# A conv and retention block on eight cores: keys of two pairs opened without the shift, loads in that order, and retention's first four chunks reordered with factors for eight heads at once

## The reference, cut to what matters

```
xm = rmsnorm(x, norm_w) * (1 + sc_x) + sh_x       # sh_x, sc_x: first two thirds of silu(c) @ ada_w + ada_b
q, k, v, gates = split(xm @ w_in)                 # the same weights for the 256 context tokens (cm)
q, k = rope2d(q), rope2d(k * 64 ** -0.5)          # 8 heads of 64; v has 8 heads of 128
s_f, s_b = states of the context's k, v           # start of the scans, forward and backward
ret = scan_forward(q, k, v, s_f) + scan_backward(q, k, v, s_b)     # chunks of 128 tokens
ret_n = (ret - mean) * rsqrt(var + eps) * gn_w    # per head
y_a = (silu(za) * bg * (conv3(cg * h) + conv_b)) @ w_a
y_b = (silu(zb) * ret_n) @ w_b
out = rmsnorm(x + g_x * ((sigmoid(ga) * y_a + sigmoid(gb) * y_b) @ w_out), final_norm_w)
```

## Time and profile before

| | us |
|---|---|
| median of 3 runs (lowest 876.34, highest 927.11) | 877.23 |
| the profiled execution's own time | 877.3 |
| its span on the slowest core (core 0) | 875.7 |
| spans of the 8 cores | 870.9 to 875.7 |
| PE busy within the span | 800.4 |
| DVE, ACT, POOL busy | 465.4, 360.7, 330.8 |

### The profile page before, as it was taken

How to read it: one execution, slowest core, us unless ns; L and a number is a source line. 1 busy time by engine, 2 the same in 40 slices (tenths; PEclk the granted TensorE clock), 3 DMA queues, 4 the chain that set the end, 5 groups by cost and what they waited for, 6 DMA issues and landing times.

```text
span 875.7 us, 14323 instructions; the slowest of 8 cores (870.9 to 875.7 us)
## 1 busy us (share of the span) xinstructions
PE 800.4 (91%) x4504; PEld 384.6 (44%) x4504; DVE 465.4 (53%) x1090; ACT 360.7 (41%) x642; POOL 330.8 (38%) x372
## 2 busy tenths in 40 slices
PE   0079999999988999999999999999999999999996
PEld 0045445444444444444444444444444444444443
DVE  2457534899778777767623442344256412333435
ACT  3589646898466435343432122122212211222222
POOL 0136523676578454545410302221143143232333
PEclk9999999999999999999999999999999999999999
DMA  8999955774391221315551715325015260034233
GB/s 244 280 290 187 212 111 97 175 156 104 55 162 35 38 54 29 55 29 78 81 86 42 118 34 96 52 46 97 1 23 122 81 112 1 25 118 148 72 120 145
DMA packets 72256, 87.83 MB, mean 100 GB/s; under 512 B 51691, under 2 KB 57963, under 8 KB 70518
## 3 DMA queue, kind: packets, MB, share of 16 engines
q1 hardware_dynamic: 66854, 59.65, 25.9%
q0 software_dynamic: 5328, 27.27, 18.9%
HBM read 93.72 MB, written 8.39 MB: 117 GB/s over the span
## 4 chain that ended last, share of the span: by engine, by line
PE 80%; DMA 6%; ACT 5%; DVE 4%; issue 3%; POOL 1%; SPq 1%; DVEq 0%; ACTq 0%; POOLq 0%
PE P L1006 53%; PE P L588 13%; PE P L1303 6%; DMA wt<-ada_w 4%; ACT tm L983 2%; DMA cm<-rope 2%; PE P L707 2%; DVE vb L1021 1%; ACT st L905 1%; PE P L828 1%; PE P L648 1%; PE P L946 1%; PE P L475 1%; PE P L691 1%; PE P L947 1%
## 5 line engine op out<-in xcount | busy, mean ns | idle before, releaser
L1006 PE MATMUL P<-xmt,vb 128*128 128x512 bf16 x1280 | 283.1, 379 | 2.8 <-DVE wt L1202 1.8
L1006 PEld LDWEIGHTS P<-xmt,vb 128*128 128x128 bf16 x1280 | 124.5, 98 | 152.6 <-issue 3.7
L588 PE MATMUL P<-wt,xmt 128*128 128x512 bf16 x688 | 158.3, 382 | 4.4 <-ACT xmt L509 3.4
L1006 PE MATMUL P<-xmt,wt 128*128 128x512 bf16 x512 | 118.8, 380 | 1.1 <-ACT wt L1157 0.9
L1205 POOL TENSOR_TENSOR kz<-tm,wt 128x1024 bf16<-128x1024 f32 x16 | 45.7, 2857 | 162.4 <-DVE wt L1202 162.4
L588 PEld LDWEIGHTS P<-wt,xmt 128*128 128x128 bf16 x688 | 65.2, 98 | 79.8 <-issue 7.5
L1006 PEld LDWEIGHTS P<-xmt,wt 128*128 128x128 bf16 x512 | 49.3, 98 | 58.3 <-issue 2.7
L1282 DVE SCALAR_TENSOR_TENSOR tm<-tm,P 128x512 f32<-128x512 f32 x32 | 22.0, 687 | 87.6 <-PE P L1006 87.6
L1158 DVE TENSOR_TENSOR wt<-P,wt 128x512 f32<-128x512 f32 x32 | 22.1, 692 | 83.4 <-ACT wt L1157 62.8
L1284 POOL TENSOR_TENSOR st<-st,tm 128x512 bf16<-128x512 bf16 x32 | 39.8, 1243 | 65.8 <-DVE tm L1282 65.8
L1006 PE MATMUL P<-vb,wt 128*128 128x512 bf16 x256 | 61.4, 386 | 0.0
(11 more groups left out here) (176 smaller groups left out, 1110.8 us busy)
## 6 DMA issues: line engine op xcount, KB each, us to landing
kz<-x SPq DMA_DIRECT2D x24, 512.0 KB, 9.2
wt<-x SPq DMA_DIRECT2D x24, 512.0 KB, 4.6
vb<-w_conv POOLq DMA_DIRECT2D x16, 512.0 KB, 8.3
out<-wt SPq DMA_DIRECT2D x15, 512.0 KB, 2.7
st<-ada_w SPq DMA_DIRECT2D x2, 2048.0 KB, 14.1
wt<-ada_w SPq DMA_DIRECT2D x2, 2048.0 KB, 28.8
vb<-w_mix POOLq DMA_DIRECT2D x8, 512.0 KB, 11.1
cm<-rope SPq DMA_DIRECT2D x33, 64.0 KB, 3.9
```

The costliest lines, as they stand in the source:

```text
L588: ins = e.matmul(pf(bank)[:, 0:wid], lhsT=lhs_x(ch, k), rhs=w[:, k, c0_:c0_ + wid], start=(k == 0), stop=(k == 7))
L1006: ins = e.matmul(pf(bank), lhsT=lhs(k), rhs=rhs(k), start=(k == 0), stop=(k == 7))
```

## The change

It has two parts; lines are those of the kernel before.

**A. The start.** The blocks of ada_w are loaded and multiplied in the order 2, 3 (scale), then 0, 1 (shift). w_k is loaded by SP as two float32 pieces (`wk_load`) and cast on DVE and ACT (`wk_cast`) instead of by one casting DMA of POOL. With the scale known and the shift not, pairs 0 and 1 are written as `xm` without the shift (`f_aff_noshift`), and their keys are begun in banks P2 to P5 (`k_open`, four chunks of 8 products). When the shift is there, it is split into two bf16 parts (`shi`), multiplied with w_k into P6 (`f_kb`, 8 products with 2 rows), split again (`kbh`, `kbl`) and added to each of the four banks by two products with ones (`k_close`). Then follow the ropes of the four chunks, and the loop begins at p = 2, where `g_acc` is called for pairs 0 and 1 both. The two columns `xmTh` that the convolution needs are made from `xh2`. The exponents of the mask are made before ada block 0 is cast (`mask_exponents`), the rest after pair 1 is opened. Loads of pairs 2, 3 and 4 follow the last ada block.

**B. Retention.** In chunks 1 to 3 the next queries' products stand in front of the scores, the first filler in front of `r_ret`, the norm is split in two around it, and only one filler is left behind `r_ret`; then `r_rtp` and `r_qtp` follow each other. In chunk 0 `r_qtp(1)` stands in front of `r_ret(0)`. `r_qtp(0)` uses bank P4 instead of P0. In all 16 chunks the factors are made for eight heads at once instead of twice for four.

SP's queue at the start, before. `ada_w` rows are blocks of 2 MB, `x` rows are chunks of 512 KB with a count, `st`, `wt`, `kz`, `xmt`, `cm` and `tm` are regions of SBUF.

The diff, cut:

```diff
+        def f_aff_noshift(pair):
+            ...
+            P.op("dve", f_d, reads=["Amod", "P0"], writes=[n_ + "d" for n_ in names])
+            P.op("act", f_a, reads=["Amod", "P1"], writes=[n_ + "a" for n_ in names])
...
+        ada_load(2)
         load2(0)
+        ada_load(3)
+        wk_load(0)
+        wk_load(1)
+        P.dma("sp", lambda e: e.dma_start(out=dpn, in_=dpn_d[:, :]), "dpn", writes=["dpn"])
+        load2(1)
+        ada_load(0)
         rope2(0)
         rope2(1)
+        ada_load(1)
+        ada_cast(2)
+        ada_mm(2, 7, 0)
+        load2(2)
+        rope2(2)
+        load2(3)
+        sq2(0)
+        scale2(0)
+        load2(4)
+        f_tp(other[0])
...
+        ada_cast(3)
+        ada_mm(3, 7, 0)
+        modT_part((1,), "modT1", 7, 0)
...
+        wk_cast(0)
+        f_aff_noshift(other[0])
+        wk_cast(1)
+        def k_open(ch, bank, part):
+            def f(e):
+                for k in range(4 * part, 4 * part + 4):
+                    ins = e.matmul(pf(bank), lhsT=lhs_x(ch, k), rhs=wk[:, k, :], start=(k == 0), stop=False)
...
+        def k_close(bank):
+            def f(e):
+                e.matmul(pf(bank), lhsT=onesb[0:2, :], rhs=kbh[0:2, :], start=False, stop=False)
+                return e.matmul(pf(bank), lhsT=onesb[0:2, :], rhs=kbl[0:2, :], start=False, stop=True)
...
+        for part in range(2):
+            for c in range(2):
+                k_open(other[0][c], 2 + c, part)
+        mask_exponents()
+        sq2(1)
+        scale2(1)
+        load2(5)
+        f_tp(other[1])
         ada_cast(0)
         ada_mm(0, 7, 0)
+        f_aff_noshift(other[1])
+        for part in range(2):
+            for c in range(2):
+                k_open(other[1][c], 4 + c, part)
+        mask_tables()
         ada_cast(1)
         ada_mm(1, 7, 0)
+        modT_part((0,), "modT", 7, 0)
...
+        P.op("dve", f_shi, reads=["modT"], writes=["shi"])
+        P.op("dve", f_slo, reads=["modT", "shi"], writes=["shi"])
...
+                ins = e.matmul(pf(6)[0:2, :], lhsT=shi[:, k, :], rhs=wk[:, k, :], start=(k == 0), stop=(k == 7))
...
+        P.op("dve", lambda e: e.tensor_copy(out=kbh[0:2, :], in_=pf(6)[0:2, :]), reads=["P6"], writes=["kbh"])
...
+        for c in range(4):
+            k_close(2 + c)
...
-        for p in range(8):
+        for c in range(2):
+            o_krope(other[0][c], 2 + c)
+        rope2(3)
+        sq2(2)
+        scale2(2)
+        o_krope(other[1][0], 4)
+        f_tp(other[2])
+        f_aff(other[2])
+        o_krope(other[1][1], 5)
...
+        for p in range(2, 8):
...
-            if p >= 1:
-                g_acc(other[p - 1], range(4), 4, p == 1, False)
+            if p == 2:
+                g_acc(other[0], range(4), 4, True, False)
+            g_acc(other[p - 1], range(4), 4, False, False)
...
+            P.op("dve", f_bna, reads=["bst0", "bst1"], writes=["bmv0", "bmv1"])
...
+            P.op("pool", lambda e: e.tensor_tensor(out=rstd8, in0=rstd8, in1=neghalf[:, 0:8], op=ALU.pow),
+                 reads=["rstd0", "rstd1", "neghalf"], writes=["rstd0", "rstd1"])
...
-        r_qtp(0)
+        r_qtp(0, 4)
...
+            if n < 4:
+                if n:
+                    r_q(n + 1, 5, rest=False)
+                r_sc(n)
+                if n:
+                    r_q(n + 1, 5, pe=False)
+                    r_norm(n - 1, (0,))
+                first_filler(n, 0)
+                if n:
+                    r_norm(n - 1, (1,))
+                else:
+                    r_qtp(1)
+                r_ret(n)
+                first_filler(n, 1)
+                if n:
+                    r_rtp(n - 1)
+                r_Fadd(n + 1)
+                if n:
+                    r_qtp(n + 1)
+                else:
+                    first_filler(0, 2)
+                continue
```

156 lines of the change are left out of this document (91 added, 65 removed).

## The result

The changed kernel takes 891.86 us (median of 4 runs, 890.38 to 892.09), the kernel before 877.16 us in the same session. The ratio is 1.0167, with a 95% interval of 1.0154 to 1.018. In some runs the cores of one die are slower as a whole at a lower granted clock; all ratios here leave such runs out. I had forecast 875.5 us, with a range of 872.0 to 880.5: the change costs 14.7 us where I had expected it to gain 1.7. It stays within 2%, as forecast, but far outside the range.

A forecast was written before the change was run, and what follows sets the result against it. PE was taken to bound all but a few places, so gains lay only where it stands still. From 877.3: start 0, early chunks -1.2, factors for eight heads -0.6, giving 875.5 us, range 872.0 to 880.5.

The forecast's parts named there:

- ACT's squares of pairs 2 and 3: Start: squares wait for x landing 3.4 and 6.7 us after the last ada block, yet finish before PE needs them.
- The landing L: Start: time the last ada block lands, forecast to move from 42.3 by +4.1 us to 46.4.
- SP is passed by nothing it needs: Start: loads of pairs 2 to 4, now queued before the last ada block's landing, keep the DMA engines busy after it.
- above 49: Start: sign of being wrong, the last ada block landing later than 49 us; below 44 was the other side.
- The chain behind L: Start: steps from the last ada block's landing to pair 2's first product, 15.5 us, ending at 61.9.
- the fast level: Start: PE's pace assumed for the eight shift products, 1.73 us instead of 3.53 at the slow level.
- a rival that had the slow one: Start: PE at its slow level when the shift arrives, with transfers 1.5 us slower; 880.0 us, chance 0.25.
- the wait at P0: Retention, chunks 1 to 3: queries' transposes wait for ACT to read bank P0; PE stands still 1.65 us.
- Chunk 4's scores: Retention: scores of chunk 4 start at 274.9 against 276.15, a term of -1.2 us.
- The power for eight heads: Retention: POOL's power for all eight heads at once takes 2.5 us, 0.6 longer, beside DVE's state addition.
- the sum of -1.8: Part B, retention: -1.2 us from the early chunks and -0.6 from factors for eight heads.
- all rivals taken together: Whole kernel: slow PE 880.0, chance 0.25; short wait at P0 872.2, chance 0.20; no effect 876.5, chance 0.15.

The follow-up runs named there:

- the chunks alone: Part B only (new chunk order, factors for eight heads) put on the kernel before, with its old start; 879.59 us, ratio 1.0027.
- The reordered start: Changed kernel with last ada block ahead of rope rows, pairs 2 and 3's scalings and pair 2's transposes and affine step moved earlier; 883.32 us, ratio 1.007.

## Why the prediction was wrong

**The step that failed** is this one of part A: "ACT's squares of pairs 2 and 3 need x that lands 3.4 and 6.7 us after L, and are done before PE asks for them by this timetable." The squares were done, 4 us after the block came. But `sq2` issues two POOL instructions per chunk as well, and I had not looked at what stands ahead of them in POOL's order. In the code written out anew, `o_krope` of pair 0 came first, and with it decay products that wait for the shift. I had listed the queues that SP was moved past, and left POOL's out. Pair 2's product came at L + 22.25, not L + 15.5; with two calls moved it comes 5.1 us earlier in the mean of the cores, and the time falls by 4.8.

**The landing L** was mis-sized: +4.1 forecast (46.4), +7.3 measured (49.57). The bytes were counted about rightly (with the order put right it is +5.1 on the slowest core and +4.6 in the mean of the cores); SP's issue was not. Three small rope rows held SP for 11.47 us, so the last ada block, of 2 MB, was issued at 24.82. With the block ahead of them it was cast at 47.35, so 2.2 of the 3.2 missing are the order (2.4 in the mean of the cores). I had given SP's order a sentence ("SP is passed by nothing it needs") and not a time. I had named "above 49" as a sign of being wrong.

**The chain behind L** held where PE's clock didn't enter: `modT_part` at L + 3.11 (forecast 3.15), the shift products at L + 3.98 (4.05), two reads at 0.68 each (0.65), the rotations 1.99 apart (1.94), the affine step 1.37 (1.36). The shift products took 3.25 us, not 1.73, so the closing began at L + 8.94 and not L + 7.5. I had chosen the fast level against a rival that had the slow one, since sixteen opened products stood "shortly before"; here they ended 5.2 us before the shift products began, with waits of 3.24 and 0.98 us between. The rival's mechanism came, but it ended at 880.0, because it counted opened, shift and closing products alone. The slow level went on with the idleness: pair 2's first products took 3.57, transposes twice 1.86, another eight products 2.78, in sum 4.2 us over the fast times between 67 and 81 us, where the granted clock was 0.53. From pair 2 to pair 3 it took 12.68 and not 7.8. The slow shift products are a consequence and not a cause of their own: with the last ada block issued ahead of the rope rows, and no edit to the products, they take 1.89 on six cores of eight, in after on one.

**What came back**: the loss was 14.45 us at pair 3 and 11.90 at the first scores. Why 2.5 are regained between them no run tested.

**Part B, the chunks**: the wait at P0 was forecast at 1.65 and measured at 1.31 to 1.47, a chunk at 9.0 and measured at 8.87; the scores' wait is gone except in chunk 4, as said. Chunk 4's scores were to gain 1.2, 0.3 of it ahead of chunk 0; from chunk 0 to chunk 4 they gained 0.57 and not 0.9, since the first chunk took 9.49 and not 8.7. The power for eight heads was forecast at 2.5 and takes 2.55 in chunk 4; the gate starts 0.46 sooner in its chain, not 0.2, but it counts at one gate and not at three. So the parts of part B were right within 0.8 us, and the sum of -1.8 was wrong by 4.2 (the chunks alone cost 2.4). Most of that are things that I had not counted at all. One is the clock: I moved a wait to stand next to another, and PE fell to 1.2 GHz behind both, 1.69 us, on five of the eight cores of the chunks alone. The other is the collision, 1.64 us and as much again for the clock behind it (2.87 between the scores), which my text had even described, in the citation on the wide power, but which I looked for at one pair of instructions only. Against them stands a gain that I hadn't counted either: before's own collision, at the second gate, is gone, 1.66 us.

**The chances**: all rivals taken together reached from 872.2 to 880.0. None was a queue behind a waiting instruction. The reordered start, which changes nothing but the order of calls, gives 8.5 of the 14.7 us back by the ratios, so the larger part of the loss is order. That the time still stayed within 2% of before, as forecast, owes nothing to the sum.

## What to carry to other kernels

- When a call is moved, write down every instruction that it issues on every engine, and for each what now stands ahead of it in that engine's order and what that waits for. The small instruction on the idlest engine (here two of under 0.6 us on POOL, which had been idle for 24 us) is the one to look for first.
- A wait of PE can cost more than itself. Here PE ran slow behind 1.47 and 1.26 us on 37 of 64 cores, and behind a single wait of 2.12 us in chunk 0 on 15 of 16, while behind a single 1.47 or 1.76 it never did: compare the durations of the same instruction behind a wait with its usual one before pricing the order of work. And where DVE and POOL both go to SBUF at the end of a stretch that PE waits for, order them by a wait: it was free here, and it made all three kernels faster that it was tried on (before, after, the chunks alone).
- Measure a change against the kernel before with such accidents removed. Before and the new chunks each had a collision at a different gate, so their plain difference (2.4 us lost) did not tell the order's own worth (nothing measurable as made, 2.3 us gained with one bank changed, 0.9949 against 0.9975).
